# First MLP product of a streaming encoder: one whole block fewer, sums of the seven products kept in PSUM

## The reference, cut to what matters

```
h2 = rms_norm(x, w_norm2)
ff = jnp.square(jax.nn.relu(jnp.einsum('bsd,df->bsf', h2, w_ff1)))   # 1024 -> 4096
x  = x + jnp.einsum('bsf,fd->bsd', ff, w_ff2)                        # 4096 -> 1024
```

## Time and profile before

| | |
|---|---|
| time, median of 3 runs | 2181.82 (2181.06 to 2183.05) |
| profiled execution, its own time | 2184.08 |
| its span, first to last instruction | 2182.3 |
| TensorE busy | 2155.8 (99%), 13154 matmuls |
| VectorE busy | 1546.5 (71%) |
| ScalarE busy | 936.9 (43%) |
| GpSimd busy | 114.5 (5%) |
| mean granted TensorE clock | 0.999 of full |
| DMA engines, mean busy share | 42% for the main queue, 151 GB/s |

### The profile page before, as it was taken

The page is one execution under the profiler, slowest core; times in us unless marked ns, Lnnn a source line. Parts: engine busy times, 40 slices in busy tenths (PEclk is TensorE's granted clock), DMA queues, the critical chain, the costliest instruction groups (busy, mean ns, idle before and its releaser), DMA issues.

```text
span 2182.3 us, 34116 instructions
## 1 busy us (share of the span) xinstructions
PE 2155.8 (99%) x13154; PEld 1931.8 (89%) x13154; DVE 1546.5 (71%) x2593; ACT 936.9 (43%) x1951; POOL 114.5 (5%) x207
## 2 busy tenths in 40 slices
PE   7999999999999999999999999999999999999998
PEld 6898788999999988888889987889999998888886
DVE  6424767888787787786863358578877787867768
ACT  5213833455555523323342158144655555223233
POOL 3300001000000000000122000010000000000002
PEclk9999999999999999999999999999999999999999
DMA  5210013344545786636312201223464549846363
GB/s 170 61 52 24 21 49 112 126 173 181 211 175 198 292 303 239 225 122 231 99 45 66 55 11 29 70 105 137 165 216 170 209 177 347 302 170 238 134 226 116
DMA packets 218001, 330.35 MB, mean 151 GB/s; under 512 B 14172, under 2 KB 104576, under 8 KB 217840
## 3 DMA queue, kind: packets, MB, share of 16 engines
q1 hardware_dynamic: 215776, 325.60, 42.1%
q0 software_dynamic: 2064, 2.57, 0.4%
HBM read 212.28 MB, written 115.64 MB: 150 GB/s over the span
## 4 chain that ended last, share of the span: by engine, by line
PE 95%; DVE 2%; DMA 1%; issue 1%; ACT 1%; POOL 0%; SPq 0%; DVEq 0%; ACTq 0%; POOLq 0%
PE ps L2169 30%; PE ps L2171 30%; PE ps L2170 30%; PE ps L2213 1%; PE ps L2322 1%; PE ps L2342 1%; DMA ff_ops<-row_op 1%; PE ps L2263 0%; PE ps L2275 0%; DMA x<-in_x_prompt 0%; PE ps L2299 0%; PE ps L2296 0%; DVE b_all L1586 0%; DVE xn L1434 0%; ACT q L953 0%
## 5 line engine op out<-in xcount | busy, mean ns | idle before, releaser
L2169 PE MATMUL ps<-h_all,w_hi 128*128 128x288 f32 (+1 forms) x1504 | 471.3, 313 | 1.5 <-DVE q L1720 1.2
L2171 PE MATMUL ps<-h_all,w_lo 128*128 128x288 f32 (+1 forms) x1504 | 470.1, 313 | 0.0
L2170 PE MATMUL ps<-h_all,w_hi 128*128 128x288 f32 (+1 forms) x1504 | 469.5, 312 | 0.0
L2169 PEld LDWEIGHTS ps<-h_all,w_hi 128*128 128x128 f32 x1504 | 282.2, 188 | 3.7 <-issue 1.8
L2170 PEld LDWEIGHTS ps<-h_all,w_hi 128*128 128x128 f32 x1504 | 282.2, 188 | 0.1
L2171 PEld LDWEIGHTS ps<-h_all,w_lo 128*128 128x128 f32 x1504 | 282.2, 188 | 0.0
L2169 PE MATMUL ps<-w_hi,h_all 128*128 128x512 f32 x576 | 232.0, 403 | 3.1 <-issue 2.9
L2171 PE MATMUL ps<-w_hi,h_all 128*128 128x512 f32 x576 | 225.6, 392 | 0.0
L2170 PE MATMUL ps<-w_lo,h_all 128*128 128x512 f32 x576 | 225.3, 391 | 0.0
L2169 PE MATMUL ps<-w_hi,ring_all 128*128 128x512 f32 x544 | 211.6, 389 | 0.0
L2170 PE MATMUL ps<-w_lo,ring_all 128*128 128x512 f32 x544 | 211.6, 389 | 0.0
(11 more groups left out here) (246 smaller groups left out, 4089.5 us busy)
## 6 DMA issues: line engine op xcount, KB each, us to landing
ff_ops<-row_op SPq DMA_DIRECT2D x128, 512.0 KB, 3.3
w_raw<-in_w_ff SPq DMA_DIRECT2D x128, 256.0 KB, 3.7
ring_all<-ff_ops SPq DMA_DIRECT2D x32, 1024.0 KB, 8.2
ring<-ff_ops SPq DMA_DIRECT2D x32, 1024.0 KB, 8.5
ff_raw<-q SPq DMA_DIRECT2D x96, 256.0 KB, 3.3
b_all<-in_w_ff SPq DMA_DIRECT2D x24, 1024.0 KB, 12.2
w_raw<-in_w_in SPq DMA_DIRECT2D x60, 256.0 KB, 3.3
ring<-ff_raw SPq DMA_DIRECT2D x12, 1024.0 KB, 5.6
```

What stands on the lines that cost most here:

```text
L2169: pe.matmul(out, sh, mh, start=first, stop=False)
L2170: pe.matmul(out, sh, ml, start=False, stop=False)
L2171: return pe.matmul(out, sl, mh, start=False, stop=last)
```

## The change

CB falls from 3 to 2: each layer has two whole blocks (`ff1(0)`, `ff1_by_depth(1)`) and 14 blocks of seven products. The products' order becomes P1, P5, P6, P2, P7, P3, P4, and four of them no longer start their sum in PSUM anew: P6, P7 and P4 go on top of P1's banks, P3 on top of P5's. Between them ScalarE copies out P1, then P5, then P1+P6 (three copies a block, not one). VectorE adds three times: C11 = P1's copy + P2, C22 = P5's copy + (P1+P6+P7), C12 = (P1+P6)'s copy + (P5+P3); C21 = P1+P6+P7+P4 lies ready in PSUM, and ScalarE's relu takes it from there. P1's banks alternate between 2, 3 and 6, 7. Product i always has slot i of `w_hi` and `w_lo`; before, the seven products walked through eight slots. The queues of ScalarE and VectorE are written out anew, and SyncE's order of loads and stores is adapted. The core of the diff, with "..." where lines are left out:

```diff
-U_KVG, U_U, U_CONV, U_Q, U_OUT, U_FF, U_END = 0, 8, 12, 24, 32, 48, 60
+U_KVG, U_U, U_CONV, U_Q, U_OUT, U_FF, U_END = 0, 8, 12, 24, 32, 48, 56
-CB = 3
+CB = 2
-FORD = ("P1", "P2", "P5", "P6", "P7", "P4", "P3")
+FORD = ("P1", "P5", "P6", "P2", "P7", "P3", "P4")
...
 SyncE
-                store_rows(1)
                 f_units(CB + 1)
-                store_rows(2)
+                store_rows(1)
                 f_units(CB + 2)
...
-                sp.wait_ge(f_used, fop(last, 2))
+                sp.wait_ge(f_used, fop(last, 1))
                 load_ring(0)
...
                 sp.wait_ge(f_used, fop(last, 5))
+                load_w2(b12, "b12", 0, 0, 512)
+                sp.wait_ge(f_used, fop(last, 6))
                 load_last(0)
                 load_w2(b21, "b21", 0, 1, 0)
-                sp.wait_ge(f_used, fop(last, 6))
-                load_w2(b12, "b12", 0, 0, 512)
...
 ScalarE, first blocks
+                f_high(CB, "P1") ... "P5", "P6", "P2"
                 rows_high(0, range(4))
                 last_high(0)
+                for pair in range(2):
+                    s_high(2, pair)
+                rows_kept(2)
+                for c in (2, 3):
                     for g in range(GROUPS):
                         relu_part(c, g)
+                copy_product(CB, "P1", 0, 0)
+                f_high(CB, "P7") ... "P3", "P4"
...
+                    if b == CB + 1:
+                        copy_product(b, "P1", 0, 0)
+                        relu_quarter(b - 1, "C12", 1, 0)
+                        f_high(b, "P7")
+                        relu_quarter(b - 1, "C21", 0, 1)
+                        f_high(b, "P3")
                         f_high(b, "P4")
+                        copy_product(b, "P5", 1, 1)
+                        copy_product(b, "P6", 1, 0)
...
 VectorE, first blocks
+                f_low(CB, "P1")
+                f_make(CB, "P5")
+                f_low(CB, "P5")
+                f_make(CB, "P6")
+                f_low(CB, "P6")
+                f_low(CB, "P2")
                 rows_low_all(0)
                 for pair in range(2):
                     s_make(2, pair)
                 for pair in range(2):
                     s_low(2, pair)
+                f_make(CB, "P7")
                 f_make(CB, "P4")
+                s_make(3, 0)
                 f_low(CB, "P7")
+                f_low(CB, "P3")
+                f_low(CB, "P4")
+                s_make(3, 1)
                 for pair in range(2):
                     s_low(3, pair)
+                for which in (1, 2, 3):
+                    rows_sum(CB - 1, which)
+                combine(CB, "C11")
+                combine(CB, "C22")
+                rows_low(CB - 1, (0, 1, 2))
+                f_low(CB + 1, "P1")
+                f_make(CB + 1, "P5")
+                combine(CB, "C12")
+                rows_sum(CB - 1, 4)
+                last_low(CB - 1)
+                f_low(CB + 1, "P5") ... f_make P6, f_low P6
+                rows_low(CB - 1, (3,))
+                f_low(CB + 1, "P2") ... f_make P7, f_low P7, f_low P3, f_make P4, f_low P4
 VectorE, every later block b
                     for which in (1, 2, 3):
                         rows_sum(b - 1, which)
+                    rows_low(b - 1, (0, 1))
+                    if more:
+                        f_low(b + 1, "P1")
+                        f_make(b + 1, "P5")
+                    rows_low(b - 1, (2,))
                     rows_sum(b - 1, 4)
                     last_low(b - 1)
+                    if more:
+                        f_low(b + 1, "P5") ... f_make P6, f_low P6
+                    rows_low(b - 1, (3,))
+                    if more:
+                        f_low(b + 1, "P2")
+                    combine(b, "C11")
+                    if more:
+                        f_make(b + 1, "P7")
+                    combine(b, "C22")
+                    if more:
+                        f_low(b + 1, "P7") ... f_low P3, f_make P4
+                    combine(b, "C12")
+                    if more:
+                        f_low(b + 1, "P4")
 TensorE, ff1_product: what a product waits for
+                    if kind == "P5":
                         pe.wait_ge(*relu_done.count((now["l"] + 1) * 2 * CB * GROUPS))
+                elif kind in ("P5", "P2"):
+                    pe.wait_ge(f_acc, acc_count(b - 1, {"P5": "C12", "P2": "C11"}[kind]))
+                elif kind == "P1" and b >= CB + 2:
+                    pe.wait_ge(f_relu, 4 * fblock(b - 1))
+                if kind in ("P6", "P7", "P3"):
+                    pe.wait_ge(f_copy, copied(b, {"P6": "P1", "P7": "P6", "P3": "P5"}[kind]))
                 if kind == "P4":
+                    pe.wait_ge(f_acc, acc_count(b, "C22"))
                 pe.wait_ge(f_lo, made(b, kind))
...
-                                      rows[:, 0, k, cols], rows[:, 1, k, cols], k == 0, k == 3)
+                                      k == 0 and kind in ("P1", "P5", "P2"), k == 3,
...
-                ff1(1)
-                ff1_by_depth(2)
+                ff1_by_depth(1)
```

More of the change, by code:

```diff
@@ L79 @@
 HG = HR // 2
[L80 to L81 removed]
+FORD = ("P1", "P5", "P6", "P2", "P7", "P3", "P4")
 FOPS = len(FORD) * SB
[L83 removed]
 FRAW = {"P1": 0, "P2": 1, "P5": 0, "P6": 0, "P7": 2, "P4": 1, "P3": 3}
[L85 to L86 removed]
+FSUM = {"P5": 1, "P6": 2, "P7": 3, "P4": 4}
+FACC = {"C11": 1, "C22": 2, "C12": 3}
+FCOPY = {"P1": 1, "P5": 2, "P6": 3}
 class Signal:
@@ L1304, in _ @@
                         s_high(which, pair)
-                relu_sq(1)
-                split(range(ids_of_w1(2), ids_of_w1(2) + 4))
+                    if which == 0:
+                        relu_sq(1)
+                f_high(CB, "P1")
+                f_high(CB, "P5")
+                f_high(CB, "P6")
+                f_high(CB, "P2")
                 rows_high(0, range(4))
                 last_high(0)
[L1310 to L1313, removed]
@@ new lines, in _ @@
+                f_high(CB, "P7")
+                f_high(CB, "P3")
+                f_high(CB, "P4")
+                for g in range(GROUPS):
+                    square_part(2, g)
+                copy_product(CB, "P5", 1, 1)
+                s_high(3, 0)
+                for g in range(GROUPS):
+                    square_part(3, g)
+                copy_product(CB, "P6", 1, 0)
+                s_high(3, 1)
+                rows_high(CB - 1, (0, 1, 2))
+                relu_quarter(CB, "C11", 0, 0)
@@ L1369, in _ @@
-                relu_quarter(FB - 1, "C12", 1, 0)
+                relu_quarter(FB - 1, "C21", 0, 1)
                 op_high(1)
@@ L2019, in _ @@
                         s_make(which, pair)
-                for pair in range(2):
-                    s_low(0, pair)
-                split(range(ids_of_w1(2), ids_of_w1(2) + 4))
-                for pair in range(2):
-                    s_low(1, pair)
+                for which in (0, 1):
+                    for pair in range(2):
+                        s_low(which, pair)
+                f_low(CB, "P1")
[4 more added lines that the diff above has]
+                f_low(CB, "P2")
                 rows_low_all(0)
@@ L2060, in _ @@
+                f_low(CB + 1, "P7")
+                f_low(CB + 1, "P3")
+                f_make(CB + 1, "P4")
+                f_low(CB + 1, "P4")
+                for b in range(CB + 1, FB):
+                    more = b + 1 < FB
                     for which in (1, 2, 3):
                         rows_sum(b - 1, which)
-                    rows_low(b - 1, (0,))
-                    combine(b, "C11")
-                    rows_low(b - 1, (1, 2))
+                    rows_low(b - 1, (0, 1))
+                    if more:
+                        f_low(b + 1, "P1")
+                        f_make(b + 1, "P5")
+                    rows_low(b - 1, (2,))
@@ L2092, in _ @@
                         for j in range(HALF):
                             op_low(0, j)
-                        for name in ("U3", "C22", "U4"):
-                            combine(b, name)
+                    combine(b, "C11")
+                    if more:
+                        f_make(b + 1, "P7")
+                    combine(b, "C22")
+                    if more:
+                        f_low(b + 1, "P7")
+                        f_low(b + 1, "P3")
+                        f_make(b + 1, "P4")
+                    else:
@@ L2096, in _ @@
                         for j in range(HALF):
                             ring_low(0, j)
-                        combine(b, "C21")
-                combine(FB - 1, "C12")
+                    combine(b, "C12")
+                    if more:
+                        f_low(b + 1, "P4")
                 for j in range(HALF):
@@ L2166, in _, with product @@
         def _(pe):
-            def product(out, sh, sl, mh, ml, first, last):
-                pe.matmul(out, sh, mh, start=first, stop=False)
-                pe.matmul(out, sh, ml, start=False, stop=False)
```

(7 more changed lines are left out.)

219 lines of the change are left out of this document (88 added, 131 removed).

## The result

The changed kernel takes 2206.24 us (median of 4 runs, 2203.34 to 2206.87), the kernel before in the same comparison 2181.88: a ratio of 1.0106 [1.0094, 1.0118]. It is slower by 24.4 us, where 15.2 were forecast. The two traced executions have spans of 2205.1 and 2182.3 us: 22.8 us more.

A forecast was written before the change was run, and what follows sets the result against it. TensorE, busy 2155.8 of 2182.3 us, was taken as the bound; savings, VectorE's delay of 9.4 us, half pace and the end summed to +7.45 and +7.75 a layer, together +15.2: 2197.0 us, range 2187 to 2207.

The forecast's parts named there:

- TensorE's own work: Per layer, a block of seven products (22.26 us) replaces a whole block (25.00 us): -2.74 us.
- old gaps: TensorE's gaps from the old queues, waiting for U2 and U3, go: -1.41 us in layer 0, -1.10 in layer 1.
- rival 3: P7 or P4 waits 0.5 us in 22 of 26 later blocks: +11 us on top, 2208; chance 10%.
- A: P5 of block 2 waits for ScalarE's relus: 2.9 us, 2.2 to 5.3 depending on store landings.
- half pace: TensorE at the lower clock level after a long gap: 1.9 us taken behind C, 0 behind A.
- gap B: At P3 and P4 of block 2, waits for VectorE cost 0.2 us together.
- C: P4 of block 3 waits for VectorE's add C22: 6.3 us, 5.2 to 7.5 depending on landings.
- floor: Had VectorE no single wait in the whole of block 3, the delay would still be 2.8 us.
- The end of the first product: Loads behind the last block asked for later, same bytes in flight: +0.3 us a layer, bounds 0 and 1.5.
- My own forecast: VectorE's delay at the start of each first product makes TensorE wait: 2197.0 us, range 2188 to 2204; chance 75%.

The follow-up runs named there:

- e5_order: Changed kernel with the same instructions in another order on VectorE and ScalarE in blocks 2 to 4; 2180.74 us, ratio 0.9990.
- e4_fill: Changed kernel with TensorE kept busy through its two gaps by 52 more matmuls a layer whose results are overwritten; 2199.45 us, ratio 1.0072.
- e1_swap: Changed kernel with block 0's splits that wait for a store moved behind the third activation sum in VectorE's queue; 2200.89 us, ratio 1.0079.
- e2_relus: Changed kernel with the last whole block's six relus ahead of a high part of the third activation sum in ScalarE's queue; 2202.72 us, ratio 1.0090.
- e6_end: Changed kernel with block 15's row sums and z_rows' operand ahead of b21's operand on ScalarE and VectorE; 2201.55 us, ratio 1.0086.
- e8_gpsimd: Changed kernel with the third activation sum computed on GpSimd instead of VectorE, queues otherwise in the same order; 2219.53 us, ratio 1.0173.
- e9_x: Kernel with the reorderings of e5_order and e6_end together, SyncE asking for x's second half right behind b22; 2185.95 us, ratio 1.0018.
- e10_traffic: Changed kernel with one useless 1 MB DRAM-to-DRAM copy more in each layer, asked for right ahead of b21; 2208.86 us, ratio 1.0121.

## Why the prediction was right, and where its size was off

**TensorE's own work and the old gaps: right.** Later blocks take 22.26 us as before, with three adds as with seven, so rival 3, a wait in every block, did not happen; without waits fourteen of them take 311.64 (e5_order, layer 1, to 0.01).

**A: right to 0.5 us in length (2.37 and 2.34 for 2.9) and to 0.22 in place.** The store landed 2.7 us after its issue, not 3.3. The half pace that follows A I set at nothing, because A is shorter than the one idle time that the rows of before had shown; it was there (P5 and P6 took 7.97 us and not 6.36), and e4_fill shows that it costs nothing in the end, since C22 doesn't wait for it. It also hid gap B, of 0.2 us: no product between A and C waits.

**C: right.** VectorE's timeline has the add C22 at 479.51 us, forecast 479.48:

```profile
478.92 0.68 DVE L1680 TENSOR_TENSOR w_raw<-w_raw 128x512 f32<-128x512 f32 x1
479.51 0.75 DVE L1748 TENSOR_TENSOR q<-ps,q 128x576 f32<-128x576 f32 x1
```

P4 follows at 480.32. Its wait is shorter than forecast (5.04 for 6.3) because TensorE was itself late by the half pace behind A. VectorE's way there fits too: the third activation sum ends at 431.69 (forecast 432.09), block 3's last low part makes way for the next operation at 466.56 (466.71). e1_swap, e2_relus and e4_fill move or remove A and leave C22's end where it was to 1.1, 0.3 and 0.6 us: A and C are one delay, as stated. The half pace behind C was 1.8 and 1.6 us, forecast 1.9. First product: +6.98 and +7.67, forecast +7.15 and +7.45.

**"Had VectorE no single wait ... that is the floor": too strong.** The floor of 2.8 us held for the order of the queue, and I let it speak for VectorE's load. e5_order does the same work with VectorE at 98 to 99% and no floor.

**The end of the first product is the term that was mis-sized:** 0.3 us a layer with bounds 0 and 1.5, measured 5.62 and 2.41 in the two traces, that is 7.4 of the 7.6 us by which the difference of their spans exceeds the forecast of 15.2. The size is uncertain: e1_swap to e4_fill, which have the same code there, stand 2.6 to 5.1 and 0.3 to 3.6 us above the kernel before. I had written that `b21` is asked for 3 us later and that the same bytes are in flight. So it was: it was issued 22.9 us after block 15's start (19.7 before), with the DMA queue at 101 to 102% of the engines' time from 740 to 800 us in both kernels by the profile, and landed 10.3 us later (9.0). But I looked for the price at the load and not at what stands behind it in two queues. ScalarE idled 6.33 us for it:

```profile
763.38 2.19 ACT L1015 ACTIVATE w_hi<-b_all 128x512 fp32r<-128x512 f32 x4 [6.33 <-DMA b_all<-in_w_ff]
765.48 0.62 ACT L992 ACTIVATE row_op<-s_one 128x512 fp32r<-128x512 f32 x1
...
768.48 1.16 ACT L1021 ACTIVATE z_all<-b_all 128x512 fp32r<-128x512 f32 x2
```

Behind it wait `z_rows`' operand and block 15's row sums, whose stores SyncE must issue before it asks for x (774.51, 22.1 us after the first product; 19.7 before). The earlier trace rows should have warned me: a wait of 0.24 us means no slack, so most of 3 us of delay had to come out; it did, as waits of 2.25 and 1.66 us. e6_end shows the first link (that `z_rows` does not wait once it is ahead of `b21`); how the rest divides between x, half pace and the traffic of that stretch is not settled to better than 2 us, since it varies by as much from run to run.

**Where luck helped.** My own forecast had the range 2188 to 2204, and 2206.24 lies above it, by the end of the first product. It lies in the whole range, 2187 to 2207, because that reaches into rival 3's lower part, and rival 3 had another cause.

## What to carry to other kernels

An engine at 98% in the stretch need not be the bound. What counts is what stands ahead of the one result that is due: cost a new wait by the queue ahead of it, and try the order before taking work away. Remove a wait only after asking whether a later one is counted from the same engine; if it is, nothing is gained. Where a wait of before is shorter than the shift that the change brings, price the shift, not the wait.

## What the runs showed of the hardware

- In the first products and the 80 us behind each, half pace followed every wait of TensorE of 2.59 us or more (up to 10.56), and none of 1.78 or less. Between them both were seen: waits of 1.81 to 2.37 us with it, and of 1.95 to 2.37 us without (2.26 in e4_fill, 2.37 in e6_end). It cost some 1.4 to 2.8 us each time. The Trainium skill (TensorE: Matmul & The Clock Gate, Part 1) has the fall of an idle array to half rate; these rows, unlike those of before, show it after full speed.
- GpSimd and VectorE in additions and subtractions of two 128x1152 operands at the same time (e8_gpsimd): VectorE's 1.36 us became 3.65 to 3.83, GpSimd's took 3.13 to 3.67, and 2.97 to 3.01 beside VectorE's splits of 128x512. The Trainium skill (GPSIMD Engine Reference, Specifications) names contention with VectorE's instructions of two SBUF inputs, which these are; the trace agrees.
- With DMA at 96% of the engines' time (e9_x) loads of 1 MB landed after 12.7 us (median of two) and a store of 256 KB after 14.1. Yet a useless copy of 1 MB (e10_traffic) made the first wait only 1.2 to 1.5 us longer.
